# A feed-forward up projection on one Trainium2 core: nine tile pairs instead of eight by seven block products

## What is computed

```
h = rmsnorm(x, ffn_norm[l])                     # 512 x 1024
u = h @ ffn_w_up[l]                             # 1024 x 5632: gate half a, value half bv
a, bv = u[..., :D_FF], u[..., D_FF:]            # D_FF = 2816
a = causal_dwconv(a, ffn_conv_w[l], ffn_conv_b[l])
x = x + (jax.nn.silu(a) * bv) @ ffn_w_down[l]
```

## Time and profile before

| | |
|---|---|
| median of 3 runs | 1967.19 us (1966.85 to 1967.53) |
| profiled execution: its time, its span | 1966.21 us, 1964.4 us |
| TensorE matmul busy | 1941.5 us, 99% of the span |
| VectorE busy, ScalarE busy | 1263.2 us (64%), 872.6 us (44%) |
| mean granted TensorE clock | 0.997 of full speed |

### The profile page before, as it was taken

One profiled execution on the slowest core, in us unless ns is written; L12 is line 12 of the kernel. 1 busy time (PEld: TensorE's weight loads), 2 busy tenths in 40 slices (PEclk: granted clock), 3 DMA queues, 4 the chain that ended last, 5 costly groups with the idle time before them and its releaser, 6 DMA issues.

```text
span 1964.4 us, 30653 instructions
## 1 busy us (share of the span) xinstructions
PE 1941.5 (99%) x11538; PEld 1630.9 (83%) x11538; DVE 1263.2 (64%) x1546; ACT 872.6 (44%) x1277; POOL 29.9 (2%) x60
## 2 busy tenths in 40 slices
PE   7999999999999999999999999999999999999998
PEld 5887888898887897888888888997777777888888
DVE  6866777877645866787887646846664644534435
ACT  5345453344323445453344322334445666544343
POOL 2001000000000001000000000000000000000000
PEclk9999999999999999999999999999999999999999
DMA  7213133333324223133333223523331222232322
GB/s 196 86 40 105 44 107 93 100 102 106 101 76 119 74 56 108 44 107 86 107 86 112 93 94 89 179 76 97 91 113 65 64 82 65 86 118 76 98 88 83
DMA packets 241077, 182.42 MB, mean 93 GB/s; under 512 B 12970, under 2 KB 232360, under 8 KB 240574
## 3 DMA queue, kind: packets, MB, share of 16 engines
q1 hardware_dynamic: 238368, 177.37, 30.4%
q0 software_dynamic: 2160, 2.22, 0.6%
q10 hardware_dynamic: 430, 1.23, 0.2%
HBM read 168.21 MB, written 2.10 MB: 87 GB/s over the span
## 4 chain that ended last, share of the span: by engine, by line
PE 88%; DVE 7%; issue 2%; ACT 1%; DMA 1%; DVEq 0%; SPq 0%; POOL 0%; ACTq 0%
PE ps L882 19%; PE ps L884 19%; PE ps L883 19%; PE ps L1421 4%; PE ps L1419 4%; PE ps L1420 4%; PE ps L669 2%; PE ps L645 2%; PE ps L658 2%; DVE amat L2238 2%; PE ps L1317 1%; PE ps L1319 1%; PE ps L1318 1%; PE ps L521 1%; PE ps L490 1%
## 5 line engine op out<-in xcount | busy, mean ns | idle before, releaser
L882 PE MATMUL ps<-h_hi,w_hi 128*128 128x512 f32 (+1 forms) x1248 | 485.6, 389 | 0.8 <-ACT qk L1624 0.4
L884 PE MATMUL ps<-h_hi,w_lo 128*128 128x512 f32 (+1 forms) x1248 | 475.8, 381 | 0.0
L883 PE MATMUL ps<-h_lo,w_hi 128*128 128x512 f32 (+1 forms) x1248 | 473.6, 379 | 0.0
L2124 DVE TENSOR_TENSOR w_lo<-w_raw,w_hi 128x2048 fp32r<-128x2048 f32 (+3 forms) x110 | 227.0, 2063 | 155.6 <-ACT w_hi L1631 148.6
L882 PEld LDWEIGHTS ps<-h_hi,w_hi 128*128 128x128 f32 x1248 | 234.6, 188 | 51.5 <-issue 7.1
L884 PEld LDWEIGHTS ps<-h_hi,w_lo 128*128 128x128 f32 x1248 | 234.4, 188 | 46.3
L883 PEld LDWEIGHTS ps<-h_lo,w_hi 128*128 128x128 f32 x1248 | 234.6, 188 | 45.0 <-issue 1.9
L1631 ACT ACTIVATE w_hi<-w_raw 128x2048 fp32r<-128x2048 f32 (+3 forms) x108 | 186.7, 1729 | 166.6 <-PE ps L1421 111.9
L2631 DVE TENSOR_TENSOR w_lo<-w_raw,w_hi 128x1024 fp32r<-128x1024 f32 (+1 forms) x118 | 126.5, 1114 | 155.5 <-ACT w_hi L1951 154.7
L882 PE MATMUL ps<-w_hi,h_hi 128*128 128x256 f32 x544 | 152.4, 280 | 0.3 <-DVE h_lo L856 0.2
L883 PE MATMUL ps<-w_lo,h_hi 128*128 128x256 f32 x544 | 150.7, 277 | 0.0
(11 more groups left out here) (437 smaller groups left out, 3397.3 us busy)
## 6 DMA issues: line engine op xcount, KB each, us to landing
w_raw<-in_ffn_w_up_dram SPq DMA_DIRECT2D x88, 512.0 KB, 4.6
w_raw<-in_w_in_dram SPq DMA_DIRECT2D x41, 1024.0 KB, 5.4
w_raw<-in_w_in_dram SPq DMA_DIRECT2D x32, 512.0 KB, 5.2
w_raw<-in_ffn_w_down_dram SPq DMA_DIRECT2D x32, 512.0 KB, 4.3
w_raw<-in_w_out_dram SPq DMA_DIRECT2D x12, 1024.0 KB, 5.0
w_raw<-in_ffn_w_down_dram SPq DMA_DIRECT2D x16, 384.0 KB, 3.6
swapped<-qk SPq DMA_DIRECT2D x96, 64.0 KB, 2.0
w_raw<-in_w_mem_kv_dram SPq DMA_DIRECT2D x4, 1024.0 KB, 4.9
```

Of the source, the lines that this page charges most:

```text
L882: pe.matmul(dst, lh, rh, start=first and j == 0, stop=False)
L883: pe.matmul(dst, lh, rl, start=False, stop=False)
L884: ins = pe.matmul(dst, ll, rh, start=False, stop=last and j == len(order) - 1)
L2124: dve.tensor_tensor(w_lo[:, slot, 0:n], w_raw[:, slot, 0:n], w_hi[:, slot, 0:n].bitcast(F32), ALU.subtract).then_inc(sem("w_split"), 1)
```

## The change

One more tile, f = 3, goes by seven products, in both layers: `FAST_FROM` is 3 instead of 5. Its weight sums are now made while VectorE works on tile 1 instead of tile 3. The token blocks were done in tiles 0, 1 and 2 (two, one and one); now they are done in tile 0 (blocks 0 and 1) and tile 2 (blocks 2 and 3), since tile 1 has the weight sums. The engines' loops start two tiles earlier and run nine times on TensorE; on VectorE and ScalarE the odd half of the first turn is written out ahead of the loop.

```diff
@@ -59,10 +59,10 @@
 
 LEVELS = (64, 32, 16, 8, 4, 2, 1)
 
-FAST_FROM, FAST_TO = 5, 19
+FAST_FROM, FAST_TO = 3, 19
 FAST = (FAST_TO - FAST_FROM) // 2 + 1
 
-BLOCKS = ((0, 1), (2,), (3,))
+BLOCKS = ((0, 1), (2, 3))
 
 CREDIT = {"w_split": 2, "tile_done": 1, "x_down": 1, "sq_sum": KD - 1, "raw_lo": KD}
 
@@ -1863,15 +1863,17 @@
                     act.wait_ge(sem("tile_copied"), upto(act, "tile_copied", T_UP + 2 * k + 2))
                     act.activation(hid_hi[:, k], hid[:, k], ACT.Copy).then_inc(sem("hid_hi"), 1)
 
-                for f, blocks in enumerate(BLOCKS):
-                    conv_start(f, f % 2)
+                def blocks_act(f, blocks):
+                    conv_start(f, 0)
                     block_copies(blocks[0])
                     conv_silu(f)
-                    up_high(f, f % 2)
+                    up_high(f, 0)
                     for j in blocks[1:]:
                         block_copies(j)
                     for j in blocks:
                         block_high(j)
+
+                blocks_act(0, BLOCKS[0])
                 f = FAST_FROM - 2
                 conv_start(f, 1)
                 act.wait_ge(sem("s_sum"), upto(act, "s_sum", 4))
@@ -1879,19 +1881,27 @@
                 conv_silu(f)
                 sums_split()
 
+                def keep_p1(n):
+                    act.wait_ge(sem("p1_done"), upto(act, "p1_done", n + 1))
+                    act.activation(sums[:, 2], ps[:, 5, 0:256], ACT.Copy).then_inc(sem("p1_kept"), 1)
+
                 def fast_act(n):
                     f = 2 * n + FAST_FROM - 1
                     conv_start(f, 0)
-                    act.wait_ge(sem("p1_done"), upto(act, "p1_done", n + 1))
-                    act.activation(sums[:, 2], ps[:, 5, 0:256], ACT.Copy).then_inc(sem("p1_kept"), 1)
+                    keep_p1(n)
                     up_high(f, 0)
                     conv_silu(f)
                     conv_start(f + 1, 1)
                     conv_silu(f + 1)
 
-                with act.Fori(0, FAST - 1) as n:
-                    fast_act(n)
-                    sums_high(2 * n + FAST_FROM, n + 1)
+                blocks_act(FAST_FROM - 1, BLOCKS[1])
+                keep_p1(0)
+                conv_start(FAST_FROM, 1)
+                conv_silu(FAST_FROM)
+                sums_high(FAST_FROM, 1)
+                with act.Fori(0, FAST - 2) as m:
+                    fast_act(m + 1)
+                    sums_high(2 * m + FAST_FROM + 2, m + 2)
                 fast_act(FAST - 1)
                 up_high(FAST_TO, 1)
                 for f in (FAST_TO + 1, FAST_TO + 2):
@@ -2534,16 +2544,18 @@
 
                 dve.wait_ge(sem("rms"), upto(dve, "rms", 4))
                 dve.wait_ge(sem("pad"), upto(dve, "pad", 1))
-                for f, blocks in enumerate(BLOCKS):
-                    gate_tile(f, f % 2)
-                    conv_taps(f, f % 2)
+                def blocks_dve(f, blocks):
+                    gate_tile(f, 0)
+                    conv_taps(f, 0)
                     block_sums(blocks[0])
-                    hidden(f, plain(f % 2))
-                    split_low(C_UP + f + 2, f % 2, KD)
+                    hidden(f, plain(0))
+                    split_low(C_UP + f + 2, 0, KD)
                     for j in blocks[1:]:
                         block_sums(j)
                     for j in blocks:
                         block_low(j)
+
+                blocks_dve(0, BLOCKS[0])
                 f = FAST_FROM - 2
                 weight_sums(f, 0, True, busy=False)
                 weight_sums(f, 0, False)
@@ -2560,8 +2572,7 @@
                     split_low(C_UP + f + 2, 0, KD)
                     hidden(f, plain(0))
 
-                with dve.Fori(0, FAST - 1) as n:
-                    fast_even(n)
+                def fast_odd(n):
                     f = 2 * n + FAST_FROM
                     gate_fast(f, n)
                     weight_sums(f, n + 1, True)
@@ -2569,6 +2580,12 @@
                     weight_sums(f, n + 1, False)
                     hidden_fast(f, n)
                     sums_low(f, n + 1)
+
+                blocks_dve(FAST_FROM - 1, BLOCKS[1])
+                fast_odd(0)
+                with dve.Fori(0, FAST - 2) as m:
+                    fast_even(m + 1)
+                    fast_odd(m + 1)
                 fast_even(FAST - 1)
                 gate_fast(FAST_TO, FAST - 1)
                 conv_taps(FAST_TO, 1)
```

## The result

The changed kernel takes 1987.34 us, the median of 5 runs (1985.73 to 1988.32), against 1966.85 us for the kernel before in the same comparison. The ratio is 1.0103, with a 95% interval of 1.0092 to 1.0114: 1.0% slower, 18 to 22 us by the interval. Predicted were 1984.8 us, 17.6 us slower, with a range of 1979.8 to 1988.4.

What follows compares the result with a forecast made beforehand. TensorE, busy 99% of the span, was taken to bound the kernel. Per layer, wait 7.9 plus clock 1.9 minus saving 1.01 gave 8.8 us, 17.6 for both, hence 1984.8 us; range 1979.8 to 1988.4.

Steps and rivals of the forecast that it cites:

- The saving, 1.01 us a layer: Tile 3 by seven products takes 9.98 us of TensorE instead of 10.99; 2.02 us over two layers.
- When TensorE asks, 293.14: In tile 3, after 24 matmuls (2.86 us) from 290.28, TensorE needs all four token blocks split.
- when the blocks are ready, 301.02: VectorE's work from 277.58 ends the last token block at 301.02, so TensorE waits 7.9 us in tile 3.
- The pieces: VectorE's four stretches before the last block: weight sums 2.86, tile 1 8.27, tile 2 8.27, block 3's sums and low parts 4.04 us.
- tile 1's sequence: VectorE's gate, taps, split, product and low weight sums for tile 1: 9.02 us less a vanished 0.75 us wait, 8.27.
- The clock: After tile 3's wait TensorE runs about 4.3 us, 20 matmuls, at 1.2 GHz; 1.9 us lost a layer, bounds 0 to 3.0.
- The rival that the clock holds: In tile 3 the clock does not fall and only the wait counts: 1981.0 us; chance 0.12.
- The rival of the loop's margin: Longer wait or successor: the loop's 0.3 us margin for split weights is overrun, tile 5 waits 0.7 us; 1989.8 us; chance 0.06.
- The sum: Tile 3 per layer: wait 7.9 plus clock 1.9 minus saving 1.01 is 8.8 us; 17.6 us for both layers.

Runs made afterwards that it cites:

- early2: `early` with VectorE's low part of the weight sums moved behind tile 2's gate and the next weights' split behind the taps; 1966.17 us, 0.9996 of the kernel before.
- ahead: Changed kernel with token blocks 2 and 3 made at the head of tile 2's work, before its gate and taps; 1974.67 us, 1.0044 of the kernel before.
- early: Changed kernel with token blocks 2 and 3 made in tile 1's work and tile 2's weights split before its gate; 1966.78 us, 1.0002 of the kernel before.
- fill66: Changed kernel with 66 useless 256-column matmuls before TensorE's wait for the token blocks in tile 3, both layers; 1980.95 us, 1.0073 of the kernel before.
- third: Changed kernel with the seventh product, which needs no token sums, made third instead of last in all nine pairs; 2003.94 us, 1.0190 of the kernel before.

## Why the prediction was right

- *The saving, 1.01 us a layer.* Right, but to be seen only without the wait: 9.97 and 9.98 us in `early2`.
- *When TensorE asks, 293.14, and when the blocks are ready, 301.02.* TensorE's 24th matmul started at 292.50 and the blocks were ready at 300.84. With one more step of 0.12 us TensorE asked at 292.62. This execution is 0.5 us ahead before the change can act (the weight sums start at 277.07 where the sum had 277.58, tile 3 at 289.78 instead of 290.28), so what lies between the dates counts. The pieces were 2.86, 8.51, 8.27 and 4.13 us where the sum had 2.86, 8.27, 8.27 and 4.04. The 0.24 us of tile 1's sequence: I let ScalarE's copy of the weights follow the start of the convolution at once, and it stood idle for 0.26 us between them (row at 281.73). The list of waits has 8.1 us where the sum had 7.9; counted as a gap in the pace of the matmuls it is 8.3. That the order on VectorE and ScalarE sets this date is shown by `ahead`, 5.3 us earlier and 5.2 us less waiting, and by `early`. The distance that the change spends, which the prediction calls nearly 20 us, is 315.14 - 296.49 = 18.7 us.
- *The clock.* It fell, as forecast, and 24 matmuls in layer 0 and 17 in layer 1 ran slow where I had 20. By comparison with `fill66` the loss is 2.3 us in layer 0 and 1.7 in layer 1; the term had 1.9 for each. The Trainium skill, "TensorE: Matmul & The Clock Gate", Part 1, says that the number of matmuls that run cold differs between runs of one kernel; here it differs between the two layers of one run. But the ground on which I took it that the clock would fall was weak, and that it came true is partly luck. The idle 2.97 us at the kernel's start began at 18.12 - 2.97 = 15.15, and the window from 15 to 20 with its 0.56 puts the fall of the clock near 15.6. So it fell 0.4 us into that idle stretch, after a stretch of thin work, and the rows did not show that 2.97 us of idle bring it down.
- *The rival that the clock holds* had its chance in the dense work before the wait. The changed kernel answers it for 8.3 us, and `ahead` for 3.0: after dense work a gap of 3.0 us between matmuls was enough, in both layers.
- *The rival of the loop's margin* is a real mechanism, but not in this kernel: `early` and `third` open it, and the changed kernel does not.
- *The sum* was 17.6 us; the two tiles show 18.8 and 18.6 us in the two profiled executions. `fill66` splits the 18.8: the wait costs 18.36 - 9.98 = 8.4 us a layer where the sum had 7.9 (0.33 of that are VectorE's pieces), and the clock 2.0 on the mean where it had 1.9. The ratios say 20.3 us (18.1 to 22.4) and 19.1 us (16.1 to 22.2), and the 18.8 lie inside both. The profiled executions differ from that of before by more, 21.3 and 20.3 us of span; 1.4 and 1.7 us of it are a slower pace of the matmuls elsewhere, below, for which the sum has no term. The time lay within the range because the range was made wide for a longer wait and a longer slow stretch, and not because this was foreseen.

## What to carry to other kernels

When work is taken off the busiest engine by preparing more on another, the price is a date: write down when the last prepared piece is asked for and add up, start to start and waits included, what stands in front of it on the preparing engine. A piece made 19 us early looks free at any place. Once it is asked for before it is there, it costs the whole delay and a slow restart of TensorE besides. Useless matmuls in the wait gave that second part back (2.3 and 1.7 us here); moving the work gave back both. And when such a wait is repaired, look at the next smallest margin, because a long wait hides it.

## What was not expected of the hardware

A run of 256-column matmuls has two paces at full clock. Windows of 30 us in which TensorE never waits, first the kernel before, then the changed kernel, then the same kernel again (the same two stretches of the program each time):

```profile
1258.00:1288.00 30.00, 30.00 (x267) 30.00 (x266) 16.67 (x20) 9.03 (x11) 0.00 (x0) 1.00 0.54 176
1925.00:1955.00 30.00, 30.00 (x267) 30.00 (x266) 14.27 (x29) 11.92 (x38) 0.00 (x0) 1.00 0.17 59
```

```profile
1277.00:1307.00 30.00, 30.00 (x267) 30.00 (x266) 16.72 (x21) 9.03 (x11) 0.00 (x0) 1.00 0.56 176
1945.00:1975.00 30.00, 30.00 (x257) 30.00 (x256) 13.82 (x27) 11.04 (x35) 0.00 (x0) 1.00 0.13 45
```

```profile
1278.00:1308.00 30.00, 30.00 (x257) 30.00 (x256) 14.92 (x18) 9.02 (x11) 0.00 (x0) 1.00 0.53 170
1945.00:1975.00 30.00, 30.00 (x267) 30.00 (x267) 14.24 (x28) 11.80 (x38) 0.00 (x0) 1.00 0.17 59
```

The number behind the first x counts the matmuls that touch the window. From start to start they are 0.113 us apart where it is 267 and 0.118 where it is 257. In one execution the slow pace came in the second stretch, in another of the same kernel in the first; by the dates of the matmuls around it, it cost 1.4 us and 1.7 us. That is about as much as the measured difference of the changed kernel, 20.3 us, lies above its two tiles, though the interval of that difference is wider than this. Of nine profiled executions it came, in one of the two stretches, in the three with a wait of 6.7 us or more (the changed kernel twice, and `third`), and in neither stretch of the six others, `ahead` with its fallen clock among them. So it isn't tied to one place of the program, and it may go with the long waits; how a wait at 293 us would slow matmuls a millisecond later the traces don't show, and the cause stays open.
